# Sixteen attention units of the prompt's last query tile move into the retention stage of a two-layer hybrid decoder step

## The reference, cut to what matters

```python
def _layer(...):
    ro, ret_new = _retention(rq, rk, heads(pr['ret_v']), ret_state)
    ro = _head_layernorm(ro, lp['ret_gn']) * jax.nn.silu(pr['ret_g'])
    o_cmp, o_sel, o_win, win_new = nsa_fn(q, _rope(q, pos), rows, win_rows, pos)
    gate = jax.nn.sigmoid(pr['nsa_gate']).reshape(B, T, 3, NSA_HEADS, 1)
    no = gate[:, :, 0] * o_cmp + gate[:, :, 1] * o_sel + gate[:, :, 2] * o_win
    no = no.reshape(B, T, NSA_WIDTH) * jax.nn.silu(pr['nsa_g'])
    go, gdn_new, conv_new = _gated_delta(...)
    mix = jnp.concatenate([ro, no, go], axis=-1)
```

## Time and profile before

| | |
|---|---|
| median of 3 runs | 2279.68 us (2278.21 to 2285.9) |
| the profiled execution's own time | 2280.29 us |
| its span | 2278.7 us |
| mean granted TensorE clock | 0.922 |
| TensorE busy (matmul) | 1985.9 us, 87% |
| VectorE, ScalarE, GpSimd busy | 982.7, 813.6, 512.9 us |
| retention, layers 0 and 1 | 294.21 to 359.79 and 1424.90 to 1490.05 us |
| delta attention, layers 0 and 1 | 359.79 to 633.00 and 1490.05 to 1763.60 us |

### The profile page before, as it was taken

How to read it: one execution, slowest core, us unless ns; L and a number is a source line. 1 busy time by engine, 2 the same in 40 slices (tenths; PEclk the granted TensorE clock), 3 DMA queues, 4 the chain that set the end, 5 groups by cost and what they waited for, 6 DMA issues and landing times. The chain is left out here.

```text
span 2278.7 us, 34709 instructions
## 1 busy us (share of the span) xinstructions
PE 1985.9 (87%) x11560; PEld 1354.8 (59%) x11560; DVE 982.7 (43%) x2408; ACT 813.6 (36%) x1894; POOL 512.9 (23%) x806
## 2 busy tenths in 40 slices
PE   6999957989968999996879999689898599999967
PEld 3644446778846676664336444567787467767633
DVE  2154355555533543443222542655654344444322
ACT  2211102334435655551222111033344366556502
POOL 0110011223243434420001100112232443444100
PEclk9999967999979999997989999689999799999979
DMA  5443111000068978853044520200000778888331
GB/s 190 157 162 118 37 41 25 1 11 1 5 162 185 211 169 205 197 131 125 0 161 149 198 80 28 51 16 1 11 1 21 182 185 181 198 208 197 92 125 42
DMA packets 173050, 242.55 MB, mean 106 GB/s; under 512 B 50714, under 2 KB 132282, under 8 KB 172192
## 3 DMA queue, kind: packets, MB, share of 16 engines
q1 hardware_dynamic: 143328, 146.81, 25.1%
q0 software_dynamic: 29536, 93.43, 15.6%
HBM read 223.23 MB, written 25.50 MB: 109 GB/s over the span
## 5 line engine op out<-in xcount | busy, mean ns | idle before, releaser
L611 PE MATMUL bank<-W,hT 128*128 128x512 f32 (+3 forms) x1152 | 444.4, 536 | 14.1 <-DMA W<-in_w_in 8.9
L611 PEld LDWEIGHTS bank<-W,hT 128*128 128x128 f32 x1152 | 213.9, 192 | 202.5 <-issue 173.3
L988 PE MATMUL bank<-XT,W 128*128 128x256 f32 (+1 forms) x768 | 246.9, 459 | 0.0
L1045 POOL DMA_DIRECT2D PS<-in_cache_nsa_kv x256 | 151.0, 590 | 270.4 <-issue 237.8
L1045 POOL DMA_DIRECT2D SHARED<-in_cache_nsa_kv x256 | 151.6, 592 | 184.5 <-DVE RP L958 103.3
L1273 ACT ACTIVATE Pr<-bank,mx 128x31 f32<-128x31 f32 (+4 forms) x192 | 85.7, 447 | 283.0 <-DVE mx L1461 282.8
L988 PEld LDWEIGHTS bank<-XT,W 128*128 128x128 f32 x768 | 136.0, 190 | 67.7 <-issue 50.4
L970 PE MATMUL bank<-CF,RP 128*128 128x128 f32 x1024 | 149.8, 295 | 24.2 <-DVE RP L958 24.0
L977 ACT ACTIVATE XT<-bank 128x512 f32<-128x512 f32 x256 | 141.1, 601 | 40.5 <-PE bank L970 40.4
L970 PEld LDWEIGHTS bank<-CF,RP 128*128 128x128 f32 x1024 | 126.6, 152 | 32.2 <-DVE RP L958 27.6
L1240 POOL TENSOR_TENSOR work<-UP,SHARED 128x512 f32<-128x512 f32 x56 | 72.9, 1307 | 249.0 <-DVE UP L1532 137.3
(11 more groups left out here) (426 smaller groups left out, 3470.8 us busy)
## 6 DMA issues: line engine op xcount, KB each, us to landing
SHARED<-in_cache_nsa_kv SPq DMA_DIRECT2D x256, 128.0 KB, 5.5
SHARED<-in_cache_nsa_kv POOLq DMA_DIRECT2D x256, 128.0 KB, 5.2
PS<-in_cache_nsa_kv SPq DMA_DIRECT2D x256, 128.0 KB, 5.5
PS<-in_cache_nsa_kv POOLq DMA_DIRECT2D x256, 128.0 KB, 5.0
W<-in_w_in SPq DMA_DIRECT2D x48, 512.0 KB, 3.7
XS<-scratch_conv_p POOLq DMA_DIRECT2D x24, 384.0 KB, 4.5
PW<-in_state_nsa_win SPq DMA_DIRECT2D x16, 512.0 KB, 3.8
Wo<-in_w_out SPq DMA_DIRECT2D x4, 2048.0 KB, 12.1
```

Of the source, the lines that this page charges most:

```text
L611: return nc.tensor.matmul(bk((c * NTILE + t) % BANKS)[:, 0:b - a], hT[:, k, t * P:(t + 1) * P], W[:, k // 2, k % 2, 0:b - a], start=(k == ...
L988: mm = nc_(self.v).tensor.matmul(out, self.v['W1'][:, kv, s, :], seg[:, s], start=(s == 0), stop=(s == SEG // PAIRS - 1))
L1045: e.dma_start(where[side * HD:(side + 1) * HD, slot, :, :], A['cache_nsa_kv'][l, page].rearrange("(p r) a g d -> p r (a g d)", r=PAIRS)[:, ...
```

## The change

The attention code becomes a class Attend that takes any list of groups (query tile, heads, branches, whether it adds to MIX). Retention makes one instance for query tile 3, branches 1 and 2: 16 units of 512 keys, in four groups of two heads. Their result is stored in MIX. Delta attention makes another for the 80 units that are left; its query tiles come in the order 2, 0, 3, 1, and those of tile 3 are the eight of branch 0, in two groups of four heads, which are added to MIX.

```diff
-    ORDER = [("front", 0), ("front", 1)]
-    for i in range(NTILE):
-        ORDER += [("back", i)] + ([("front", i + 2)] if i + 2 < NTILE else []) + [("norm", i)]
+    STEPS = [("turn", 0), ("att", 0), ("turn", 1), ("att", 1), ("back", 0), ("turn", 2), ("att", 2), ("norm", 0), ("rows", 0), ("back", 1), ("turn", 3),
...
+    heads = Attend.groups_of(EARLY_TILE, (1, 2), False)
+    NU = sum(len(g[1]) * len(g[2]) for g in heads)
+    ORDER, u = [("unit", 0), ("unit", 1)], 2
+    for j, step in enumerate(STEPS):
+        ORDER.append(step)
+        while u < NU and u < (NU + 1) * (j + 1) / len(STEPS) + 1:
+            ORDER.append(("unit", u))
+            u += 1
+    ORDER += [("unit", k) for k in range(u, NU + Attend.BACK)]
...
-    QM = sb(scope, "QM", [P, 2, NB, 64])
-    VM = sb(scope, "VM", [P, NB, 256])
+    QM = [U[hp][:, NQ:NQ + 512].rearrange("p (b c) -> p b c", b=NB) for hp in range(2)]
+    VM = [U[2 + k][0:64, NQ:NQ + 512].rearrange("p (b c) -> p b c", b=2) for k in range(2)]
...
+            for what, i in ORDER:
+                if what == "unit":
+                    attend.pool_unit(e, i)
...
+                if what == "state":
+                    q, hp = divmod(i, 2)
+                    dve.wait(e, f"ss{i-1}m" if i else f"s1{TILES[1]}")
+                    if hp == 0:
+                        dve.wait(e, f"vm{q}")
+                    for k in range(2):
+                        mm = nc.tensor.matmul(bk(SU, 4)[:, 2 * k:2 * k + 2, :], KDc_[0:64, 0, hp * P:(hp + 1) * P], VM[k][:, :, hp * P:(hp + 1) * P],
                                               start=True, stop=True)
...
+    def pe_unit(self, e, u):
+        if u < self.NU:
+            self.scores(e, u)
+        if u >= self.BACK:
+            self.values(e, u - self.BACK)
+        if 1 <= u <= self.NU:
+            self.turn(e, u - 1)
...
+EARLY_TILE = 3
+JOINT_TILES = (2, 0, 3, 1)
...
-    QTS, BRANCHES, DEEP, BACK, AHEAD = (3, 0, 1, 2), (1, 2, 0), 2, 3, 0.95
...
+    heads_of = sum([Attend.groups_of(EARLY_TILE, (0,), True) if qt == EARLY_TILE else Attend.groups_of(qt, (1, 2, 0), False) for qt in JOINT_TILES], [])
+    AHEAD, BACK = 0.95, Attend.BACK
+    cost = [2 * P + (NCP if br == 0 else (qt + 1) * P) for qt, hs, brs, adds in heads_of for h in hs for br in brs]
```

More of the change, by code:

```diff
@@ L708, in retention @@
-    for what, i, t in ORDER:
-        if what == "front":
-            dn += [f"{x}{t}" for x in ("qk", "att0", "att1", "kd")]
-            dn += ["qm0", "qm1", "vm"] if t == 4 else []
-            pn += [f"T{t}", f"a{t}"]
+    cps = []
+    for kv in range(2):
+        HT = sb(scope, "HTp", [HD, 64])
+        HS = sb(scope, "HSp", [HD, G, 32])
+        cps.append(Compress(v, 2, PG, RP, XT, HT, HS, KC, VC, ".p"))
+        cps[kv].HALVES, cps[kv].SECOND, cps[kv].TURNS, cps[kv].own = (0, 1), (0, 1), 0, True
@@ L802, in _ @@
-            for what, i, t in ORDER:
+            for what, i in ORDER:
+                if what == "unit":
+                    attend.pe_unit(e, i)
+                    continue
+                t = TILES[i]
                 u, n = U[t], ROWS[t]
                 QK, ATT, KDc = QK_[:, i % 2], ATT_[:, i % 2], KDc_[:, i % 2]
-                if what == "norm":
-                    beside(what, i)
-                if what == "front":
+                if what == "rows":
+                    dve.wait(e, f"att1{TILES[2]}")
+                    for k in range(2):
+                        cps[0].transposes(e, pe, act, dve, k)
+                if what == "halves":
+                    if i == 0:
+                        e.wait_ge(small, 13 * 16)
+                        dve.wait(e, f"att1{TILES[4]}")
+                    cps[i].halves(e, pe, act, i)
+                if what == "second":
+                    dve.wait(e, "A1.p")
+                    for kv in range(2):
+                        cps[kv].second(e, pe, act, dve, kv)
+                if what == "turn":
@@ L854, in _ @@
-                beside(what, i)
+                    pe.done(e, f"sv{i}", mm)
         @block.vector
@@ L994, in half_copy @@
         pe.wait(e, f"H{kv}{self.seq}")
-        if kv:
+        if kv and not self.own:
             dve.wait(e, f"A0{self.seq}")
@@ L1257, in _ @@
                     mask(*mask_after[what, x])
-                if what == "unit" and x >= BACK and (x - BACK) % GROUP == GROUP - 1:
-                    merge((x - BACK) // GROUP)
+                if what == "unit":
+                    attend.pool_unit(e, x)
             dve.wait(e, "n33")
@@ L1348, in _ @@
                 if what == "unit":
[L1349 to L1354 removed]
+                    attend.pe_unit(e, x)
                     continue
```

525 lines of the change are left out of this document (288 added, 237 removed).

## The result

The changed kernel takes 2329.9 us (median of 4 runs, 2325.27 to 2334.92) against 2280.6 us: a ratio of 1.0215, 95% interval 1.0194 to 1.0235. The forecast was 2292 with a range up to 2308. Slower was right, the size was four times too small: +49 us instead of +12.

The account below looks back on a forecast made before the run. Delta attention mostly bound by TensorE's queue, retention by TensorE and VectorE waiting in turn at low clock. Per layer +31 retention, -24 delta attention: +7, two layers +14, rounded down by 2; 2279.7 + 12 = 2292 us, range 2281 to 2304.

Parts of the forecast that it names:

- the walk: Retention's new order followed for where TensorE stands: 17 us of standing, the stage growing by 31 us.
- surcharge: Retention: extra time because part of TensorE's work runs at the lower clock level, 13 us.
- the head: Start of retention: TensorE stands 4 us for first exponentials and VectorE copies; 8 us of work at half level.
- the two places named: Retention's long waits, ahead of the turn of the rows and of the third state product: 5 us each.
- the tail: End of retention: last units drain, then ScalarE's copy and GpSimd's merge; TensorE stands 2 to 3 us.
- The table loads: ScalarE loads its table three times over retention and delta attention instead of once, at no cost.
- I take 8 us of TensorE's work at half level in the head and 2.5 behind each of the waits: 13 us on top: Retention: clock starts low until the first dense stretch and may fall at each 5 us wait; 13 us added.
- My upper bound: Retention's largest growth, the whole stage at half level as now: some 43 us.
- I take 3 us for more time at the lower level: Delta attention: 3 us lost to lower clock, from 27 of 36 us saved, leaving a saving of 24.
- The floor of the levels: Delta attention's plain levels: their own chain takes some 4.8 us, so shrinking a unit there saves at most 0.3 to 0.7.
- C: Rival: delta attention hardly shortens, clock falls and chain sets pace; saving 17, retention +36, 2318 us; chance 0.08.
- A: Rival: units' dense work keeps retention's clock high; retention 84 us, 27 saved in delta attention, 2262 us; chance 0.25.

Follow-up runs that it names:

- e6: Changed kernel with extra TensorE products in both long stands of retention (four each) and near its end (one and three): 2289.5 us, ratio 1.0049.
- e3: Changed kernel with four extra 512-column products in each of retention's two long stands: 2300.0 us, ratio 1.0081.
- e11: Control: changed kernel with eight extra 512-column products a layer right behind the two long stands instead of in them: 2316.4 us, ratio 1.0168.
- e12: Changed kernel with only the second long stand filled, four products ahead of the third state product: 2304.2 us, ratio 1.0106.
- e2: Changed kernel's delta attention (80 units) behind the old kernel's retention, the sixteen early units left out: 2247.9 us, ratio 0.9863.
- e13: Changed kernel with long stands shortened and fills in retention and delta attention's first steps, none ahead of its groups: 2276.1 us, ratio 0.9987.
- e15: Changed kernel without its sixteen early units, long stands shortened and remaining ones filled: 2237.3 us, ratio 0.9806.
- e14: Kernel before with fills in retention and in delta attention's first steps, none ahead of its groups: 2269.5 us, ratio 0.9962.
- e7: Kernel before with fills on TensorE in the stands of its retention, no early units: 2273.2 us, ratio 0.9976.
- e5: Changed kernel with four extra 512-column products a layer near retention's end, long stands left empty: 2304.7 us, ratio 1.0091.
- e8: Changed kernel with second-half masked values in own memory, written earlier, and rows laid out ahead of the first norm: 2292.8 us, ratio 1.0058.
- e4: Changed kernel with eight early units in retention instead of sixteen, the other eight run in delta attention: 2312.5 us, ratio 1.0141.

## Why the prediction missed

**The direction and the walk: right.** Retention was to be TensorE's work at full clock plus stands plus surcharge plus join, 65 + 17 + 13 + 1 = 96 us. Layer 0 had 66.4 + 19.6 + 20.6 = 106.6: the work from e6, the stands as the span less TensorE's 86.98 us, the surcharge as the rest. The stands were 2.6 in the head (for 4), 4.51 and 5.5 at the two places named (for 5 and 5), and 1.65 and 4.41 in the tail with the join (for 4 together); the rest is small. The table loads cost nothing, as said. The one ahead of Silu stands directly between two ScalarE instructions and took 1.28 us, with no drain beside it; TensorE didn't wait for it:

```profile
385.14 0.22 ACT L1223 ACTIVATE HTp<-bank 64x64 f32<-64x64 f32 x1 [2.71 <-PE bank L1214]
385.38 1.28 ACT L1239 ACT_TABLE_LOAD   x1
386.67 0.58 ACT L1239 ACTIVATE HSp<-HSp,B 64x62 f32<-64x62 f32 x2
```

**The step that failed: "I take 8 us of TensorE's work at half level in the head and 2.5 behind each of the waits: 13 us on top".** The surcharge was 20 to 22 us (86.98 and 88.58 busy, less 66.4). By the stretches at 0.50 above and the factor of 1.76 of the earlier trace rows, an estimate, it lay elsewhere than I had it: 3 us in the head instead of 8, 2 behind the first wait, close to 2.5, but 7.7 behind the second instead of 2.5, and 7 from 379.5 us to the end of the stage, for which the sum had no term. Both large ones are borne out by the same products at full clock (21.8 us against 14.3 in e3, 16.7 against 9.5 in e11). I had read the fall after 338.88 in the earlier trace rows as an event of a few us because the stage ended soon after; but the earlier trace rows showed 340 to 350 at 0.50 with TensorE busy for 6.53 of 10, and the 10 us behind it stood at 0.50 as well: the last third of the old retention was one such spell (the row is below). And I counted on units to lift the clock because they are dense by busy time; they did not within 20 us. My upper bound, a growth of 43 for the whole stage at half level, was too low besides: 65 us of work times 1.76 are 114 us without any stand.

```profile
350.00:360.00 10.00, 6.07 (x28) 5.38 (x28) 5.16 (x17) 0.81 (x3) 0.00 (x0) 0.50 0.04 7
```

**The second failure: "I take 3 us for more time at the lower level" in delta attention.** The two terms of its saving, 36 - 9 for the levels and -3 for the clock, can be read apart. To hold against the earlier trace rows, layer 1 of the kernel before:

```profile
1490.00:1762.00 272.00, 243.89 (x1855) 210.28 (x1855) 149.44 (x358) 106.23 (x365) 73.12 (x91) 0.95 0.04 10
```

TensorE's idle time grew from 29.7 to 33.9 us in layer 0 and from 28.1 to 34.5 in layer 1: 4 to 6 us, where I had 9 of the 36 not saved. Its busy time should have fallen by 36 and fell by 19 and 21, since what was left took longer: 15 to 17 us for the clock, where I had 3. The saving was 15, not 24. So the two errors went opposite ways, and it is partly luck that 24 was no further off. The floor of the levels holds where it was read: 4.81 us for an estimate of 4.8.

That the clock sets this is seen in other runs too. The same program of 80 units, cut at its last unit, took by granted clock: 261.5 us at 0.87 (e12), 258.4 at 0.88 (after), 256.7 at 0.89 (e3), 252.3 at 0.91 and 250.5 at 0.92 (e2), 248.4 at 0.93 (e3, layer 1). That is 2 us for each hundredth, with TensorE idle for 33 to 35 us in each; continued to 0.96 it would be some 242 us, an estimate beyond what was measured.

**The rivals.** C, with its mark "once the clock of delta attention goes below 0.90", came nearest: saving 15 for its 17, retention +42 for its +36, 2330 us for its 2318. I gave it 0.08, because I weighed it by delta attention's dense parts. Its second half, that the chain of the levels sets the pace, did not come: TensorE's idle time grew by 4 to 6 us only. A, a high clock, can be had in retention, but not by the units: e13 is A's retention (84 for 84) by shortened stands and fills. Its +20 there against -23 in delta attention gives 2275 us (median 2276.1), not 2262, because delta attention stayed at 0.93 and 0.92.

**What the change is worth.** With stands shortened and filled, sixteen units cost retention 23.5 us a layer (e13 against e15) and free 22 to 26 in delta attention (e13 against e14 and e7): 2276.1 us against 2273.2 (e7) and 2269.5 (e14), by the ratios 0.9987, 0.9976 and 0.9962, whose intervals overlap. So no gain is shown, and no clear loss. The two stages aren't alike: the filled old retention takes 60 us for 29 us of work at full clock, so 36 us of units can enter for 23.5, and delta attention is nearly full. What is missing for a gain is the clock: delta attention with 80 units ran at 0.93 and 0.92 in e13, and with 96 at 0.96 and 0.97 in e14. Without the care for stands the change loses 49 us; 54 lie between it and e13. The fastest kernel here that leaves nothing out is the one before with fills, e14, by 0.01 to 0.74% against the kernel before, which hardly stands out from e7.

**What stays open.** Whether delta attention inherits a low clock from retention (e5's layers disagree), or falls because its work is thinner, or because its query tiles come in another order: no run kept the old order with 80 units. Whether it could be held at 0.96 with 80 units, which by the estimate above would be worth some 7 us a layer. Why the same short stand is followed by a spell in one program and not in another. And why executions of one program differ by several us.

## What to carry to other kernels

Price a wait of the matmul engine by the granted clock of the stretch behind it, not by its own length: here 6 us of waits cost 11 to 13 in their stage, and 18 a layer by the medians. Ahead of a move of work, price both places at the clock that they will have afterwards: the place that takes the work gets new waits, and the place that gives it away can run at a lower level, which here took back 15 to 17 of 36 us. Filling a wait with throw-away products paid where the wait was several us long; fills larger than the stands go onto the path (14.8 us against 5.9).

## What the runs showed of the hardware that I had not expected

- A spell at 1.2 GHz of 20 us with TensorE busy for 87 and 92% by the profile, and another with a window of 100%, in a mix of products of 64 to 512 columns. Four products of 512 columns in a row behind the same wait ended it within some 7 us (e11), and put into the wait they kept it from beginning (e3).
- The stand need not be long, but a short one doesn't decide: 1.65 us ahead of the values at 379.51 was followed by 20 us at 0.50, and in e8 by low clock from 367 us on; in e11 (1.64 us) the clock stayed at 1.00. In e6, with a fill there, the stand was 0.79 and the windows from 350 to 390 all have 1.00.
- Adding instructions shortened the program: e3's eight products a layer made it 30 us faster, e5's four at the end of the stage 25, e11's in the wrong place still 11 to 13.
- Taking work away can cost clock: delta attention with eight units fewer (e4) took 2 to 5 us longer, at 0.86 instead of 0.96.
